# Scale and gate of an expert's output: one VectorE operation out of PSUM in place of one on ScalarE and one on GpSimd

## The reference, cut to what matters

```python
g, idx = lax.top_k(aff.T, cap)            # cap: 64 latent and 16 context tokens for each expert
xe = xt[idx]
h = silu(xe @ w_gate) * (xe @ w_up)       # each 1024 x 1024
ye = (h @ w_down) * g[..., None]
out = zeros_like(xt).at[idx].add(ye)
xs = xs + ms[5] * out                     # ms[5]: a gate for each feature
```

## Time and profile before

| what | value |
| --- | --- |
| median of three runs | 2017.0 us (2015.63, 2017.0, 2023.64) |
| the profiled execution's own time | 2014.45 us |
| its span | 2012.6 us |
| busy: PE, DVE, ACT, POOL | 1787.1, 1551.8, 1213.0, 604.3 us |
| length of one step, from one `hidden` to the next | 35.86 us |
| steps | 32 in all, of which 28 fetch rows |

### The profile page before, as it was taken

The page is one execution under the profiler, slowest core; times in us unless marked ns, Lnnn a source line. Parts: engine busy times, 40 slices in busy tenths (PEclk is TensorE's granted clock), DMA queues, the critical chain, the costliest instruction groups (busy, mean ns, idle before and its releaser), DMA issues.

```text
span 2012.6 us, 26468 instructions
## 1 busy us (share of the span) xinstructions
PE 1787.1 (89%) x8919; PEld 1223.6 (61%) x8919; DVE 1551.8 (77%) x1791; ACT 1213.0 (60%) x1536; POOL 604.3 (30%) x349
## 2 busy tenths in 40 slices
PE   5899789699999999999588788896899999999996
PEld 2677667466666666566276566675566656666563
DVE  2666653599999999999275499635799999999994
ACT  2576611287777777777242156412677777777773
POOL 2132610214344343452110241101034345343431
PEclk9899897699999999999789789995899999999997
DMA  9532035699999999999710510016799999999992
GB/s 322 211 131 84 1 136 216 258 360 363 378 355 379 368 368 374 356 379 365 254 69 1 192 65 1 1 55 260 257 359 367 373 357 378 368 369 378 355 381 60
DMA packets 141088, 518.46 MB, mean 258 GB/s; under 512 B 8799, under 2 KB 17279, under 8 KB 141022
## 3 DMA queue, kind: packets, MB, share of 16 engines
q1 hardware_dynamic: 132768, 489.46, 63.7%
q0 software_dynamic: 6880, 22.75, 5.0%
q10 hardware_dynamic: 1374, 5.37, 0.7%
HBM read 496.31 MB, written 21.24 MB: 257 GB/s over the span
## 4 chain that ended last, share of the span: by engine, by line
PE 52%; DVE 21%; issue 16%; ACT 5%; DMA 3%; POOL 2%; SPq 1%; DVEq 0%; POOLq 0%; ACTq 0%
PE ps L817 20%; PE ps L821 10%; DVE whl L1559 9%; PE ps L775 6%; PE ps L1020 4%; ACT whl L1179 2%; DVE W L1590 2%; PE ps L751 1%; DMA ring<-in_mod_w 1%; PE ps L849 1%; DVE W L1577 1%; DVE W L1837 1%; PE ps L706 1%; PE ps L743 1%; PE ps L924 1%
## 5 line engine op out<-in xcount | busy, mean ns | idle before, releaser
L1559 DVE TENSOR_TENSOR whl<-ring,whl 128x1024 fp32r<-128x1024 f32 x768 | 969.8, 1301 | 78.5 <-ACT whl L1179 65.9
L1179 ACT ACTIVATE whl<-ring 128x1024 fp32r<-128x1024 f32 x768 | 805.3, 1058 | 252.8 <-PE ps L821 247.0
L817 PE MATMUL ps<-whl,xs_hl 128*80 128x512 f32 x2048 | 561.2, 396 | 7.3 <-DVE xs_hl L1583 3.8
L817 PEld LDWEIGHTS ps<-whl,xs_hl 128*80 128x80 f32 x2048 | 298.7, 149 | 169.3 <-issue 6.0
L821 PE MATMUL ps<-whl,xs_hl 128*80 128x512 f32 x1024 | 323.0, 397 | 10.8 <-DVE whl L1559 7.5
L817 PE MATMUL ps<-whl,hs_hl 128*80 128x512 f32 x1024 | 280.6, 396 | 3.4 <-ACT hs_hl L1090 3.4
L602 POOL TENSOR_TENSOR W<-W 80x1024 f32<-80x1024 f32 x32 | 100.2, 3130 | 482.3 <-ACT W L1217 482.3
L821 PEld LDWEIGHTS ps<-whl,xs_hl 128*80 128x80 f32 x1024 | 147.5, 148 | 113.0 <-DVE whl L1559 37.9
L817 PEld LDWEIGHTS ps<-whl,hs_hl 128*80 128x80 f32 x1024 | 153.2, 150 | 89.2 <-ACT hs_hl L1090 3.8
L821 PE MATMUL ps<-whl,hs_hl 128*80 128x512 f32 x512 | 160.8, 396 | 0.0
L597 POOL COPY si<-idx_t 80x1 uint32 (+1 forms) x32 | 127.9, 3997 | 0.0
(11 more groups left out here) (268 smaller groups left out, 2602.6 us busy)
## 6 DMA issues: line engine op xcount, KB each, us to landing
ring<-in_moe_w_gate SPq DMA_DIRECT2D x128, 1024.0 KB, 7.2
ring<-in_moe_w_up SPq DMA_DIRECT2D x128, 1024.0 KB, 6.8
ring<-in_moe_w_down SPq DMA_DIRECT2D x128, 1024.0 KB, 6.6
ring<-in_mod_w SPq DMA_DIRECT2D x48, 1024.0 KB, 9.6
ring<-in_rg_w_in SPq DMA_DIRECT2D x8, 1024.0 KB, 12.1
ring<-in_at_w_qkv SPq DMA_DIRECT2D x8, 768.0 KB, 20.1
x_hat<-r ACTq DMA_DIRECT2D x2, 2560.0 KB, 19.1
ring<-in_rg_w_out SPq DMA_DIRECT2D x4, 1024.0 KB, 7.7
```

What stands on the lines that cost most here:

```text
L817: nc.tensor.matmul(ps[0:CE, bank + n, :], xhl[:, part, k, :], w[:, 0, n * 512:(n + 1) * 512], start=(k == 0 and part == 0), stop=False)
L1179: nc.scalar.activation(whl[:, q % HL, 0, :], ring[:, slot, (q % 2) * D:(q % 2 + 1) * D], ACT.Copy).then_inc(whi_ok, 1)
L1559: v.tensor_tensor(whl[:, q % HL, 1, :], ring[:, n % MSLOTS, (q % 2) * D:(q % 2 + 1) * D], whl[:, q % HL, 0, :].bitcast(F32), ALU.subtract) ...
```

## The change

`output` moves from ACT to DVE and becomes one instruction that reads PSUM, multiplies by `sg` (a value for each partition) and by `gg` (a tensor), and writes `ob`. ACT's instruction, POOL's multiplication and the semaphore between them go away. DVE does it behind its subtraction of block 20 (in the last step, behind block 7), and first waits for PE to have used block 15 (in the last step, block 7) and for `sg`. POOL then only waits for `ob_ok` and issues the scatter.

```diff
@@ POOL, body
-                    pool.wait_ge(y_act, e + (base + 1))
-                    nc.gpsimd.tensor_tensor(ob[0:CE, :], ob[0:CE, :], gg[0:CE, :], ALU.mult).then_inc(ob_ok, 1)
                     pool.wait_ge(ob_ok, e + (base + 1))
@@ ACT
-                def output(e):
-                    act.wait_ge(sg_ok, e + (base + 1))
-                    nc.scalar.activation(ob[0:CE, :].rearrange("p (h n) -> p h n", h=2), ps[0:CE, 4:6, :], ACT.Copy,
-                                         scale=sg[:, 0:1]).then_inc(y_act, 1)
...
-                        if q == 20:
-                            output(e)
@@ DVE
+                def output(e):
+                    eng.wait_ge(whl_used, block_of(layer, e, 15 if not isinstance(e, int) or e < NE - 1 else 7))
+                    eng.wait_ge(sg_ok, e + (base + 1))
+                    v.scalar_tensor_tensor(out=halves(ob[0:CE, :]), in0=ps[0:CE, 4:6, :], scalar=sg[:, 0:1], in1=halves(gg[0:CE, :]),
+                                           op0=ALU.mult, op1=ALU.mult).then_inc(ob_ok, 1)
...
                         rest(layer, e, par, q)
+                        if q == 20 and more:
+                            output(e)
...
+                    if not more:
+                        output(e)
```

More of the change, by code:

```diff
@@ L265, in build @@
         h_ok, htr_mm, hh_ok, hl_ok = sem("h_ok"), sem("htr_mm"), sem("hh_ok"), sem("hl_ok")
-        whi_ok, wlo_ok, whl_used, y_act = sem("whi_ok"), sem("wlo_ok"), sem("whl_used"), sem("y_act")
+        whi_ok, wlo_ok, whl_used = sem("whi_ok"), sem("wlo_ok"), sem("whl_used")
         ob_ok, sg_ok, gi_ok, si_ok = sem("ob_ok"), sem("sg_ok"), sem("gi_ok"), sem("si_ok")
@@ L1226, in body @@
                                 h_high(e)
-                        act.wait_ge(whl_used, block_of(layer, e, 7))
-                        output(e)
                         return
```

## The result

The changed kernel takes 2036.7 us (median of five runs, 2033.02 to 2044.84). The kernel before, timed with it, takes 2017.73 (2015.63 to 2023.64). The ratio is 1.0107, with a 95% interval of 1.0088 to 1.0125: slower by 1.1%. I had forecast 1983 us, faster by 1.7%. In the sign and in the size the forecast was wrong.

The account below looks back on a forecast made before the run. DVE's gapless chain from `x_mod` to `hidden`, for which PE waits, was taken to set the step (35.86 to 34.9 us). Savings of 28.0 + 1.2 + 4.4 = 33.6 us gave 1980.9, plus 2.5: 1983 us, range 1975 to 1999.

Parts of the forecast that it names:

- the last of the change's parts: Scatter inside a step, on POOL: issued about 1.1 us earlier, the gather behind it keeps its distance; no term.
- Rival 2: POOL's scatter descriptors and copies fall on a DVE subtraction between `x_mod` and `hidden`; about 2012 us; chance 0.06.
- the 2.20 us: DVE's loss at block 21's subtraction beside POOL's multiplication, to be regained in each of 28 steps.
- PE's waits as two: PE in a step: waits 0.27 us before a block's low part and 0.56 us before `h_turn`, for `hidden`.
- the long subtraction: DVE's subtraction of block 21: 3.42 us against a median of 1.218, put down to POOL's multiplication.
- rival 3: DVE's block 21 subtraction is long for another reason than POOL and stays; 2046 us; chance 0.05.
- The new operation: DVE's added 80 x 1024 operation, between `x_mod` and `hidden`: 1.20 us, netting 1.00 us saved in each of 28 steps.
- The ends of the mixtures: Scaling to scatter issue after the last step, twice: 2.2 us saved each time, 4.4 us in all.
- The full sum: Whole kernel: 33.6 us off the profiled 2014.45 gives 1980.9, plus 2.5 for the timed median, 1983 us.
- Rival 1: Memory becomes the bound: DMA at 369 GB/s lets a step shrink only to 35.7 us; 2007 us; chance 0.08.
- the 10.1 us: From the gather's issue on POOL to its use at the next `x_turn`, against a landing of about 7 to 8 us.
- The exclusion that the prediction leaned on: GpSimd and DVE operations with two SBUF inputs share a port pair; the loser waits for the whole instruction.

Follow-up runs that it names:

- `gather_first`: Changed kernel with POOL issuing the next gather, now three experts ahead, straight behind the scatter's issue, before the landing wait and copies: 1982.23 us, ratio 0.9825.
- `late_ahead`: Changed kernel with DVE's operation of expert e - 1 behind `hidden` of expert e, and POOL's gather, three experts ahead, before the scatter: 1963.67 us, ratio 0.9727.
- `no_output`: Changed kernel without DVE's new operation, so nobody scales or gates and the scatter adds zeros after DVE's block 20: 1958.74 us, ratio 0.9711.
- `act_kept`: Changed kernel plus a useless 80 x 1024 copy on ACT at the place of its old scaling: 2043.56 us, ratio 1.013.
- `act_late`: Changed kernel plus two useless ACT copies behind `x_high`, meant to make block 22's high part late: 2041.72 us, ratio 1.0139.
- `pool_dummy`: Changed kernel plus a useless 80 x 1024 multiplication on POOL between DVE's new operation and the scatter: 2102.17 us, ratio 1.0424.
- `dve_gap`: Changed kernel with DVE waiting behind its new operation until POOL's queue has passed the scatter: 2005.94 us, ratio 0.9949.

## Why the prediction was wrong

**The failed step** is the last of the change's parts: "The scatter inside a step is issued about 1.1 us earlier ... It keeps its distance ... No term." It was issued earlier, and its issue then took 9 to 14 us in most steps in place of 1.56. The reason that I gave for the distance, that POOL's small copies get through when DVE turns to `hidden`, was taken from one step, where the `sg` copy does so (782.46 in the earlier trace rows), and not asked of the scatter itself, nor of the two copies behind `sg`, which were held up for 4.58 and 4.20 us in the same trace. The term that belongs there is +54.5 us (2036.7 against `gather_first`'s 1982.2): in the profiled executions 41.5 us more of waits in front of `x_turn` (47.0 against 5.5), and 29 us more PE busy time for the same matmuls (1800.8 against 1771.7), the share of the lower clock, of which some is given back where other waits get shorter.

**The rival that named the place.** Rival 2, with 0.06, said that POOL's other SBUF work would fall on the chain. It had the right pair of instructions and the wrong loser: it let DVE pay, half of the 2.20 us, and ended at 2012 us. It was POOL that paid, DVE's chain was never touched, and PE paid through the gather. I argued against it with one row, the scatter at 774.85, whose issue ran beside `x_rest` and six subtractions at 1.56 us. That row showed that the two can run side by side in that order of events, behind a POOL multiplication that had just held DVE. It did not show that they always do. The prediction also reads PE's waits as two where there are three: the low part of block 21 (775.13) comes some 0.3 us late as well. No term hangs on that.

**What was right.** POOL's multiplication was the cause of the long subtraction, and it went (the most is 1.27 us; rival 3 is out). The new operation costs 1.19 to 1.20 us in the chain (605.36 to 606.56), against 1.20. The step without a late gather is 35.07 us in the changed kernel (414.00 to 449.07) and 34.85 in `gather_first`, against 34.9. The ends of the mixtures give back 2.3 us each (2.09 from the scaling's start to the issue, against 4.38), against 2.2. The full sum, 1980.9 and 2.5, is met by `gather_first` with 1982.2. Rival 1 is out as well: `late_ahead` runs ten steps at a mean of 387 GB/s, where the earlier trace rows had 369.

**Where the slack was.** In the kernel before, the gather is issued 10.1 us before its use and takes 7 to 8 to land. So 2 to 3 us of delay on POOL were free. A long issue is 12.1 us longer than the old one; 8.4 us of that come back, since the small copies are no longer held up, and the 4.5 us by which the gather is later in the step above are still more than was free. I had written the 10.1 us down, and had priced neither a longer issue nor the copies' delay, which is also why so little was free.

**What stays open.** Which instant lets POOL in. In the trace of after, the issues of the steps end 1.4 us (the length of an issue alone, within 0.06) behind the start of a DVE instruction, all thirty of them: fifteen behind `h_rest` (607.50 + 13.67 = 621.17 against 619.78), six behind `hidden`, five behind a subtraction and four, the short ones, behind `x_rest`. So POOL gets in there at the border between two DVE instructions, and what is open is why it is passed over at up to eleven borders before that one. The issues of `late_ahead` do not end so: 632.33 + 4.10 - 1.40 = 635.03 lies within its `h_rest` (634.65 to 635.46). `no_output` gets in at `x_rest`, 0.2 us after its issue began, as close as in `act_kept`, where the issue took 13.66 us. That POOL is let in where DVE's next instruction is not yet released fits the short issues of `act_late`; its step at 595.76 is not in keeping with it, since block 22 was released only about when `x_rest` began. What is shown is that with DVE's new operation ahead of block 21 the way is closed in most steps, and that a delay of 0.76 us ahead of block 21 or a gap behind `x_rest` opens it. A scatter from another engine's queue than POOL's was not tried.

## What to carry to other kernels

When an operation leaves a slow engine, look at what stands behind it in that engine's list and who waits for the last item, not only at the operation: here a gather with 2 to 3 us of slack stood behind the scatter, its landing and three small copies. A transfer that is wanted soon should be issued ahead of one that nobody waits for; that order cost nothing where it wasn't needed (1.0004) and brought 54 us where it was. And an operation added to the engine that sets the pace belongs behind the result that others wait for: behind `hidden` the same 1.27 us were free. A row that shows two engines side by side without harm shows it for that order of events alone.

## What the runs showed of the hardware that I had not expected

- An indirect DMA's issue on POOL takes 1.40 us alone and up to 13.71 beside a gapless run of DVE operations of 0.8 to 1.3 us each; an 80 x 1024 multiplication on POOL took 14.88 us there, and a copy of 80 values 6.39. POOL can lose to a whole run of short instructions, not only to the one that is running. The kernel before shows it already: its `si` copy takes 4.58 us in most steps, and 0.17 in the kernel after. The Trainium skill, page "SBUF — State Buffer", section "Who interferes with whom", says that a DVE operation with two SBUF inputs contends with a GpSimd instruction that reads SBUF, and infers that it leaves descriptor generation alone. Beside `tensor_tensor` subtractions the measured issues took up to 13.7 us, which goes against the inference as far as an indirect issue is concerned; whether it waited for its descriptors or for reading its row numbers in `si`, no run tells apart.
- The exclusion that the prediction leaned on works in both directions: the same POOL multiplication held DVE for 2.20 us in the kernel before, and was held by it for 12.6 us (14.88 against 2.33) in `pool_dummy`.
- 0.76 us of pause on DVE, over before the issue begins, are enough to bring the issue down to 2.44 us (`dve_gap`).
- After a PE wait of 2.54 us the granted clock was 0.50 for the next 6 us, after one of 2.12 us (at 785.10) it was 1.00; from `x_turn` to the end of the second block it took 6.25 us (637.74 to 643.99), where by the 1.38 us a block and 0.55 for the turn of the prediction it is 3.3. The slower clock costs that step more than the wait did.
